# Ten unused TensorE products left out of the attention units of a hybrid decoder layer

## The chip, the cores and the metric

The kernel runs on one core of a Trainium2 chip. The metric is the device time of one execution in microseconds (us). The kernel before took 753.51 us, the median of three runs (752.41 to 755.99). The span of its profiled execution, from the first to the last instruction, is 749.3 us.

## The reference

One layer: a combined input projection feeds a state-space head group (S5) and a sparse attention head group; both are normalised, joined and projected out; a gated MLP with a short convolution follows. Cut to the part around the change:

```python
def one_block(args):                       # one block of 128 queries
    s_h = jnp.einsum('bthd,bsd->bths', qib, ki)
    s_idx = jnp.einsum('bths,bth->bts', jax.nn.relu(s_h), wib)
    _, sel = lax.top_k(s_idx, topk)        # 128 keys of up to 512
    logits = jnp.einsum('bthd,btkhd->bhtk', qb, kg) * scale
    p = jax.nn.softmax(logits, axis=-1)
    return jnp.einsum('bhtk,btkhd->bthd', p, vg)
...
y_ssm = _s5_mixer(u, ...)                  # diagonal state space, gelu, gated by a 512x512 product
y_mix = jnp.concatenate([_rmsnorm(y_ssm, ...), _rmsnorm(y_attn, ...)], axis=-1)
h = h + g1[:, None, :] * (y_mix @ w_out)
hn2 = _modulate(_rmsnorm(h, norm_ffn), sh2, sc2)
h = h + g2[:, None, :] * ((jax.nn.gelu(gate) * val) @ w_down)
```

The sequence has 512 positions, the model 1024 channels, and there are 8 heads of 64.

## The kernel before, in words

Each engine has its program written out by hand, in an order fixed in the source, and semaphores tie the engines together. The large float32 products (lines 1601 to 1603, `mm3`) are split into a high and a low part of each operand. Up to about 180 us the program makes the projections. Then come 32 attention units, number i being head i % 8 of query tile i // 8, with 128, 256, 384 or 512 keys by tile. After them come the output projection (to about 360 us) and the MLP.

A unit has these steps: TensorE forms the logits (line 1816, into bank i % 2); VectorE adds the mask and takes the maximum (line 1368); ScalarE takes the exponential (line 962); TensorE turns the probabilities (line 1606, `flip`, into bank 2 + i % 2); ScalarE copies them back (line 935); TensorE multiplies them with the values (line 1836). VectorE's program also holds, between its two mask steps of a pair of units and those of the next, the rounds of the top-k search for a later tile (lines 1309 and 1312), parts of S5, and later the sums of the modulation vectors (line 1175). The table `S5_AT` puts the S5 stages among the units: "u" (turns of 64x64), "lags" (line 1927), "states" (line 1917), "y" (lines 1946 and 1951), "g" and "glu".

TensorE's loop takes two units at a time: the logits of units i and i + 1, and then, for the units i - 2 and i - 1, the S5 stage, the turn of the probabilities, and the values of the unit before. The logits of unit i wait until VectorE has read those of unit i - 2 from the same bank (`logit_ready`). The table `KEEP_BUSY` names ten even units, 8 to 22 and 28 and 30. Ahead of the logits of such a unit TensorE makes one more product (line 1969, `keep_busy`): the identity as the one operand, 512 columns of the turned keys as the other, into the bank of the turned probabilities. It waits for no semaphore, sets none, and nobody reads what it writes before the next turn overwrites it. Two more of this sort of product in other places (`warm`, line 1642, in the first 40 us; lines 2062 and 2068 in `up_first`, behind 340 us) are not touched.

Of the kernel before, what the change touches and what calls it, by code (L numbers as in the profile page):

```python
# [96 lines left out]
    return ((t,),) * ROUNDS.get(i, 0), ((t,) if i < 24 and i % HEADS == 7 else ())  # L97


KEEP_BUSY = (*range(8, 24, 2), 28, 30)  # L100
OUT_BANK = ((4, 6, 7, 5), (0, 1, 2, 3))
LOGITS = 3
LO_DVE = U_GLU
# [2 lines left out]
def layer(nc, x, c, positions, w_ada, b_ada, norm_mix, w_in, ssm_log_dt, ssm_a_re, ssm_a_im, ssm_b_re,  # L106
# [6 lines left out]
    with ExitStack() as ctx:  # L113
        def sb(name, shape, dt=F32, stack=ctx):
            return stack.enter_context(nc.sbuf_tensor(name, shape, dt))
# [4 lines left out]
        bank = [ctx.enter_context(nc.psum_tensor(f"bank{i}", [P, 512], F32)) for i in range(8)]  # L120
# [6 lines left out]
        ident = sb("ident", [P, P])  # L127
# [23 lines left out]
        def cut(a, *shape):  # L151

            n = math.prod(shape)
            assert a + n <= ARENA
            v = arena[:, a:a + n]
            names = "abcd"[:len(shape)]
            if len(shape) == 1:
                return v
            return v.rearrange(f"p ({' '.join(names)}) -> p {' '.join(names)}",
                               **{k: s for k, s in zip(names, shape)})  # L160
# [3 lines left out]
        q_t, k_t = cut(0, 4, SEQ), cut(2048, 4, SEQ)  # L164
# [1431 lines left out]
        def _(pe):  # L1596
            T = nc.tensor
# [213 lines left out]
            def logits(i):  # L1811
                t, h = i // HEADS, i % HEADS
                hp = slice(64 * (h % 2), 64 * (h % 2) + 64)
                if i >= 2:
                    pe.wait_ge(S["logit_ready"], i - 1)
                T.matmul(bank[i % 2][:, 0:KEYS[t]], q_t[hp, h // 2, t * P:(t + 1) * P], k_t[hp, h // 2, 0:KEYS[t]],
                         start=True, stop=True).then_inc(S["logit_mm"], 1)

            def turn_probs(i):
                t = i // HEADS  # L1820
                pe.wait_ge(S["prob_ready"], i + 1)
                if i >= 2:
                    pe.wait_ge(S["prob_t_ready"], i - 1)
                for s in range(t + 1):
                    ins = flip(bank[2 + i % 2][:, s * P:(s + 1) * P], prob[:, i % 2, s * P:(s + 1) * P])
                ins.then_inc(S["prob_turned"], 1)

            def values(i):
                t, h = i // HEADS, i % HEADS
                pe.wait_ge(S["prob_t_ready"], i + 1)  # L1830
                if h == 0:
                    pe.wait_ge(S["proj_read"], 16 + t + 1)
                if h == 0 and t >= 2:
                    pe.wait_ge(S["y_attn_ready"], t - 1)
                for s in range(t + 1):
                    ins = T.matmul(bank[4 + t % 2][:, h * HD:(h + 1) * HD], prob_t[:, i % 2, s * P:(s + 1) * P],  # L1836
                                   v_tok[:, s, h * HD:(h + 1) * HD], start=(s == 0), stop=(s == t))
                ins.then_inc(S["pv_done"], 1)
# [125 lines left out]
                    ins = flip(bank[b][:, t * P:(t + 1) * P], y[:, t, (k % 4) * P:(k % 4 + 1) * P])  # L1964
                ins.then_inc(S["mix_t"], 1)

            def keep_busy(i):

                T.matmul(bank[2 + i % 2][:], ident[:], k_t[:, 0, :], start=True, stop=True)

            for i in range(0, ATT_UNITS + 4, 2):
                if i < ATT_UNITS:
                    if i in KEEP_BUSY:
                        keep_busy(i)
                    logits(i)
                    logits(i + 1)
                for j in (i - 2, i - 1):
                    if j in S5_AT:
                        s5(*S5_AT[j])
                    if 0 <= j < ATT_UNITS:  # L1980
                        turn_probs(j)
                    if 0 <= j - 1 < ATT_UNITS:
                        values(j - 1)
# [199 lines left out]
```

## Time and profile before

| | us |
|---|---|
| median of three runs | 753.51 |
| lowest and highest run | 752.41, 755.99 |
| span of the profiled execution | 749.3 |
| TensorE busy | 703.0 |
| VectorE busy | 458.9 |
| ScalarE busy | 338.4 |
| mean granted clock of TensorE | 0.983 |

The profiled execution is a single one; the span runs from its first to its last instruction, and the page gives no time of its own for what lies around it. The median is 4.2 us above the span. TensorE's time is start to modelled end of its instructions, so that a busy TensorE is not one at its peak. The granted clock is a share of 2.4 GHz: 1.00 is 2.4 GHz, 0.50 is 1.2 GHz, and a value between them is a stretch that holds some of both.

### The profile page before, as it was taken

The page shows a single profiled execution, that of the slowest core. Times are in us where ns is not written, and L with a number is a line of the kernel's source. Part 1 is how long each engine was busy: PE and PEld are TensorE (multiplying, and loading weights), DVE is VectorE, ACT ScalarE, POOL GpSimd, SP SyncE. Part 2 cuts the span into 40 slices and gives each one's busy share as a digit, 9 for nine tenths or more (in the row PEclk, how much of TensorE's full clock was granted, in tenths as well). Part 3 has the DMA queues.
Part 4 walks back from the last instruction along what each step waited for, and adds up shares of the span by engine and source line. Part 5 has one row for each costly group of instructions (what it writes and reads, how often), then busy time and mean ns, then how long its engine had stood idle before and what let it go on. Part 6 is the DMA issues. An engine that isn't in the chain of part 4 may idle for free.

```text
span 749.3 us, 9903 instructions
## 1 busy us (share of the span) xinstructions
PE 703.0 (94%) x3570; PEld 554.8 (74%) x3570; DVE 458.9 (61%) x817; ACT 338.4 (45%) x508; POOL 262.9 (35%) x212
## 2 busy tenths in 40 slices
PE   0799999999888899999899999999999999999997
PEld 0587777777575566888797888888878887888886
DVE  2868987976999899798615866654554544000005
ACT  4534456746522756423665445455545454122120
POOL 2002899329904200000023343443342443443440
PEclk9999999999879999999998999999999999999999
DMA  8952221260373738645603323313313313313302
GB/s 335 380 138 74 66 103 57 85 197 1 39 75 73 234 133 314 246 170 194 227 1 113 99 69 112 112 59 109 111 58 112 110 59 113 108 61 112 113 1 112
DMA packets 63081, 91.46 MB, mean 122 GB/s; under 512 B 12011, under 2 KB 41475, under 8 KB 62980
## 3 DMA queue, kind: packets, MB, share of 16 engines
q1 hardware_dynamic: 59520, 89.44, 37.2%
q10 hardware_dynamic: 3523, 1.54, 0.7%
q8 instruction: 22, 0.36, 0.2%
q14 instruction: 16, 0.12, 0.1%
HBM read 86.28 MB, written 4.69 MB: 121 GB/s over the span
## 4 chain that ended last, share of the span: by engine, by line
PE 68%; DVE 24%; ACT 3%; issue 3%; DMA 1%; SPq 0%; DVEq 0%; ACTq 0%
PE bank L1601 20%; PE bank L1603 20%; PE bank L1602 20%; DVE arena L1175 4%; DVE w_lo L1161 2%; PE bank L1606 2%; DVE arena L1312 2%; DVE arena L1151 2%; DVE stat L1309 2%; PE bank L1951 1%; DMA xh<-in_x 1%; PE bank L1946 1%; DVE arena L1368 1%; PE bank L1836 1%; ACT w_hi L697 1%
## 5 line engine op out<-in xcount | busy, mean ns | idle before, releaser
L502 POOL TENSOR_TENSOR w_lo<-w_raw,w_hi 128x2048 fp32r<-128x2048 f32 x33 | 152.1, 4612 | 349.5 <-ACT w_hi L1047 280.3
L1601 PE MATMUL bank<-act_hi,w_hi 128*128 128x512 f32 (+2 forms) x384 | 148.1, 386 | 2.1 <-DVE conv L1557 1.6
L1602 PE MATMUL bank<-act_lo,w_hi 128*128 128x512 f32 (+2 forms) x384 | 147.0, 383 | 0.0
L1603 PE MATMUL bank<-act_hi,w_lo 128*128 128x512 f32 (+2 forms) x384 | 146.8, 382 | 0.0
L1601 PE MATMUL bank<-w_hi,act_hi 128*128 128x512 f32 x240 | 98.5, 410 | 1.1 <-DVE act_lo L1201 1.1
L1603 PE MATMUL bank<-w_hi,act_lo 128*128 128x512 f32 x240 | 94.9, 396 | 0.0
L1602 PE MATMUL bank<-w_lo,act_hi 128*128 128x512 f32 x240 | 94.6, 394 | 0.0
L697 ACT ACTIVATE w_hi<-w_raw 128x2048 fp32r<-128x2048 f32 x26 | 49.8, 1913 | 84.8 <-PE bank L1603 82.1
L1601 PEld LDWEIGHTS bank<-act_hi,w_hi 128*128 128x128 f32 x384 | 73.1, 190 | 17.9 <-issue 2.0
L1553 DVE SCALAR_TENSOR_TENSOR conv<-bank,vec_cols,conv 128x511 f32<-128x511 f32 x44 | 33.0, 749 | 86.2 <-ACT conv L1057 85.8
L1603 PEld LDWEIGHTS bank<-act_hi,w_lo 128*128 128x128 f32 x384 | 73.1, 190 | 14.4
L1602 PEld LDWEIGHTS bank<-act_lo,w_hi 128*128 128x128 f32 x384 | 73.2, 191 | 14.3 <-issue 0.2
L1601 PE MATMUL bank<-w_hi,ff_hi 128*128 128x512 f32 x176 | 69.6, 396 | 0.0
L1603 PE MATMUL bank<-w_hi,ff_lo 128*128 128x512 f32 x176 | 69.5, 395 | 0.0
L1602 PE MATMUL bank<-w_lo,ff_hi 128*128 128x512 f32 x176 | 69.5, 395 | 0.0
L1591 DVE TENSOR_TENSOR up<-bank,arena 128x512 f32<-128x512 f32 x8 | 5.5, 692 | 103.5 <-PE bank L1603 103.5
L1057 ACT ACTIVATE conv<-bank,vec_cols 128x512 f32<-128x512 f32 x44 | 33.9, 778 | 72.9 <-PE bank L1603 72.9
L1606 PE MATMUL bank<-ident,arena 128*128 128x128 f32 (+1 forms) x252 | 39.5, 281 | 20.4 <-DVE arena L1139 11.4
L1601 PEld LDWEIGHTS bank<-w_hi,act_hi 128*128 128x128 f32 x240 | 45.2, 188 | 17.1 <-issue 7.5
L1566 DVE TENSOR_TENSOR up<-conv 128x512 f32<-128x512 f32 x22 | 42.4, 1964 | 19.8 <-ACT conv L1064 19.7
L1603 PEld LDWEIGHTS bank<-w_hi,act_lo 128*128 128x128 f32 x240 | 45.1, 188 | 10.6
L1606 PEld LDWEIGHTS bank<-ident,arena 128*128 128x128 f32 (+1 forms) x252 | 29.2, 144 | 31.9 <-issue 15.2
(318 smaller groups left out, 1176.8 us busy)
## 6 DMA issues: line engine op xcount, KB each, us to landing
w_raw<-in_w_up SPq DMA_DIRECT2D x44, 512.0 KB, 4.6
arena<-in_w_ada SPq DMA_DIRECT2D x18, 1024.0 KB, 8.2
w_raw<-in_w_down SPq DMA_DIRECT2D x22, 512.0 KB, 4.2
w_raw<-in_w_in SPq DMA_DIRECT2D x10, 1024.0 KB, 5.1
xh<-in_x SPq DMA_DIRECT2D x8, 512.0 KB, 7.4
w_raw<-in_w_out SPq DMA_DIRECT2D x4, 1024.0 KB, 10.1
arena<-in_w_ada SPq DMA_DIRECT2D x2, 2048.0 KB, 11.3
arena<-lag_dram SPq DMA_DIRECT2D x16, 128.0 KB, 5.5
```

What stands on the lines that cost most here:

```text
L502: nc.gpsimd.tensor_tensor(w_lo[:, slot, 0:width], w_raw[:, slot, 0:width], w_hi[:, slot, 0:width].bitcast(F32), ALU.subtract).then_inc(S[" ...
L697: nc.scalar.activation(w_hi[:, slot(n), 0:width], w_raw[:, slot(n), 0:width], ACT.Copy).then_inc(S["hi_ready"], 1)
L1057: nc.scalar.activation(conv[:, q, :], bank[q][:], ACT.Identity, scale=vec_cols[:, bass.ds(j * 2 + (C_W2 + f), 1)], bias=vec_cols[:, bass.d ...
L1151: ins = V.scalar_tensor_tensor(dst, src, silu_c[:, k:k + 1], dst, ALU.mult, ALU.add)
L1161: V.tensor_tensor(w_lo[:, slot(n), :], w_raw[:, slot(n), :], w_hi[:, slot(n), :].bitcast(F32), ALU.subtract).then_inc(S["lo_ready"], 1)
L1175: link(V.scalar_tensor_tensor(acc, src, s, acc, ALU.mult, ALU.add), "ada_used" if k == 3 else "dve_chain")
L1553: V.scalar_tensor_tensor(conv[:, q, 1:], bank[q][:, 0:SEQ - 1], vec_cols[:, bass.ds(j * 2 + (C_W1 + f), 1)], conv[:, q, 1:], ALU.mult, ALU ...
L1566: V.tensor_tensor(up32[:, q, :], conv[:, q, :], conv[:, 2 + q, :], ALU.mult).then_inc(S["ff32_ready"], 1)
L1601: T.matmul(dst, lhs_hi, rhs_hi, start=start, stop=False)
L1602: T.matmul(dst, lhs_hi, rhs_lo, start=False, stop=False)
L1603: return T.matmul(dst, lhs_lo, rhs_hi, start=False, stop=stop)
L1606: return T.matmul(dst, src, ident[at:at + n, at:at + n], is_transpose=True, start=True, stop=True)
```

## The change

The table `KEEP_BUSY`, the function `keep_busy` and its call are taken out. TensorE's program is otherwise the same, and so are those of the other engines; line numbers behind the table are one lower, and behind the function seven lower.

```diff
-KEEP_BUSY = (*range(8, 24, 2), 28, 30)
 OUT_BANK = ((4, 6, 7, 5), (0, 1, 2, 3))
...
-            def keep_busy(i):
-
-                T.matmul(bank[2 + i % 2][:], ident[:], k_t[:, 0, :], start=True, stop=True)
-
             for i in range(0, ATT_UNITS + 4, 2):
                 if i < ATT_UNITS:
-                    if i in KEEP_BUSY:
-                        keep_busy(i)
                     logits(i)
                     logits(i + 1)
```

TensorE's program of the kernel before around unit 16, where L1917 is the stage "states", L1816 the logits of units 16 and 17, and L1946 and L1951 the stage "y":

```order
L1917 MATMUL bank<-up,s_mem 64x64 x32
L1606 MATMUL bank<-ident,arena 128x128 x2
L1836 MATMUL bank<-arena 128x64 x2
L1969 MATMUL bank<-arena,ident 128x512
L1816 MATMUL bank<-arena 128x384 x2
L1946 MATMUL bank<-arena,s_mem 64x128 x2
```

The same place of the changed kernel, with its line numbers:

```order
L1916 MATMUL bank<-up,s_mem 64x64 x32
L1605 MATMUL bank<-ident,arena 128x128 x2
L1835 MATMUL bank<-arena 128x64 x2
L1815 MATMUL bank<-arena 128x384 x2
L1945 MATMUL bank<-arena,s_mem 64x128 x2
```

Only the row of L1969 is gone. The last two of the ten stand ahead of the logits of units 28 and 30; before:

```order
L1836 MATMUL bank<-arena 128x64 x4
L1969 MATMUL bank<-arena,ident 128x512
L1816 MATMUL bank<-arena 128x512 x2
L1606 MATMUL bank<-ident,arena 128x128 x4
L1836 MATMUL bank<-arena 128x64 x4
L1606 MATMUL bank<-ident,arena 128x128 x4
L1836 MATMUL bank<-arena 128x64 x4
L1969 MATMUL bank<-arena,ident 128x512
L1816 MATMUL bank<-arena 128x512 x2
```

And after:

```order
L1835 MATMUL bank<-arena 128x64 x4
L1815 MATMUL bank<-arena 128x512 x2
L1605 MATMUL bank<-ident,arena 128x128 x4
L1835 MATMUL bank<-arena 128x64 x4
L1605 MATMUL bank<-ident,arena 128x128 x4
L1835 MATMUL bank<-arena 128x64 x4
L1815 MATMUL bank<-arena 128x512 x2
```

Nothing between them changes its place.

## Rows read from the trace of the kernel before

**Rows 1.** The page, busy tenths in 40 slices of the span.
```profile
DVE  2868987976999899798615866654554544000005
PEclk9999999999879999999998999999999999999999
```

**Rows 2.** All records of line 1969 (two of each product): least, median, longest ns.
```profile
L1969 PE MATMUL bank<-arena,ident x20: 592/648/1167, 189.2 to 294.0; 128*128 128x512 f32 x20
```

**Rows 3.** VectorE in order of time: start, duration, what, [idle before <- releaser].
```profile
192.38 0.48 DVE L1368 CUSTOM_DVE_ANT_0 arena<-bank,arena,stat 128x256 f32<-128x256 f32 x1 [0.91 <-PE bank L1816]
...
249.79 0.62 DVE L1368 CUSTOM_DVE_ANT_0 arena<-bank,arena,stat 128x384 f32<-128x384 f32 x1 [0.87 <-DVE arena L1312]
...
263.01 1.29 DVE L1424 TENSOR_TENSOR act_lo<-bank,act_hi 128x512 fp32r<-128x512 f32 x2 [1.48 <-ACT act_hi L883]
...
296.01 0.75 DVE L1368 CUSTOM_DVE_ANT_0 arena<-bank,arena,stat 128x512 f32<-128x512 f32 x1 [0.55 <-PE bank L1816]
```

**Rows 4.** The chain that ended last, where line 1969 is in it: start, us.
```profile
189.37 1.81 PE bank L1969 x2
...
247.90 0.91 PE bank L1969 x2
```

**Rows 5.** Stretches: length, busy PE, PEld, DVE, ACT, POOL; granted clock; DMA share, GB/s.
```profile
202.00:203.00 1.00, 0.07 (x1) 0.00 (x0) 0.93 (x4) 0.00 (x0) 0.92 (x2) 1.00 0.80 173
203.00:204.00 1.00, 0.00 (x0) 0.00 (x0) 0.96 (x4) 0.00 (x0) 1.00 (x1) 1.00 1.26 154
205.00:206.00 1.00, 1.00 (x9) 0.88 (x9) 0.97 (x2) 0.00 (x0) 0.00 (x0) 0.84 1.26 119
209.00:210.00 1.00, 1.00 (x10) 1.00 (x9) 0.93 (x3) 0.00 (x0) 0.00 (x0) 0.95 1.16 114
219.00:220.00 1.00, 1.00 (x15) 1.00 (x14) 1.00 (x2) 0.42 (x1) 0.00 (x0) 0.67 0.98 208
226.00:227.00 1.00, 1.00 (x7) 0.64 (x5) 1.00 (x2) 0.00 (x0) 0.92 (x2) 0.92 1.24 110
188.00:189.00 1.00, 1.00 (x11) 1.00 (x9) 0.93 (x4) 0.80 (x4) 0.92 (x2) 0.81 0.00 0
184.00:188.00 4.00, 2.31 (x18) 1.74 (x19) 2.87 (x12) 4.00 (x10) 3.92 (x3) 1.00 0.00 0
260.00:264.00 4.00, 2.31 (x20) 2.13 (x19) 2.45 (x6) 3.24 (x6) 0.00 (x0) 1.00 1.01 378
```

**Rows 6.** TensorE in order of time, "states" at either clock, and idle ahead of "u".
```profile
211.17 2.10 PE L1917 MATMUL bank<-s_mem 128*64 128x64 f32 x64
...
218.82 1.57 PE L1606 MATMUL bank<-ident,xh 64*128 64x64 f32 x16 [1.79 <-DVE arena L1407]
...
221.69 3.74 PE L1917 MATMUL bank<-up,s_mem 128*64 128x64 f32 x64
```

**Rows 7.** TensorE in order of time, around unit 16 and the stage "y".
```profile
226.39 1.08 PE L1969 MATMUL bank<-arena,ident 128*128 128x512 f32 x2
227.47 1.31 PE L1816 MATMUL bank<-arena 64*128 64x384 f32 x4
230.36 0.44 PE L1946 MATMUL bank<-arena,s_mem 128*64 128x128 f32 x4 [1.58 <-DVE s_mem L1407]
```

**Rows 8.** TensorE in order of time, around units 22, 28 and 30.
```profile
261.61 1.42 PE L1606 MATMUL bank<-ident,arena 128*128 128x128 f32 x11 [1.53 <-ACT arena L977]
...
293.56 1.08 PE L1969 MATMUL bank<-arena,ident 128*128 128x512 f32 x2
294.85 1.79 PE L1816 MATMUL bank<-arena 64*128 64x512 f32 x4 [0.22 <-DVE stat L1368]
```

**Rows 9.** The chain of waits, first and last TensorE pieces between 294 and 306 us.
```profile
294.85 1.79 PE bank L1816 x4
...
305.47 0.45 PE bank L1606 x4
```

**Rows 10.** The chain of waits, last TensorE piece of "y".
```profile
246.56 0.58 PE bank L1951 x8
```

## The prediction

> **What bounds the kernel now.** The change touches only the attention units, from about 180 to 306 us, so I read the page's slices first. There the reader is to see VectorE at seven to nine tenths, where from 400 us on it stands at four to six, and TensorE's granted clock below nine tenths in two slices [rows 1]. VectorE is the engine that the units wait for, and TensorE has slack, so a product taken from it pays only where VectorE waits. The second view is all records of line 1969: 20 records for ten products, median 648 ns each [rows 2]. In a row one product keeps TensorE 1.08 us at full clock [rows 7, 8], and 1.81 us of the chain at half clock in the one at 189 us [rows 4]. Together that is 9 x 1.08 + 1.8 = 11.5 us of TensorE's time, which is not what the change can give. The third view is VectorE in order of time: in 120 us it waits with a gap worth naming only at 192.38 (0.91 us), 249.79 (0.87), 263.01 (1.48) and 296.01 (0.55) [rows 3]. The chain that ended last holds two of the ten products, ahead of the first two of these waits, with 1.81 and 0.91 us [rows 4]. The fourth view is the granted clock by stretch. It is at its lower level, 1.2 GHz, from 205.7 to 209.1 us (0.84 in the first slice is 0.32 us at the lower level, 0.95 in the last is 0.10 us) and from 219.3 to 226.2 (0.67 and 0.92), that is for 3.4 and 6.8 us [rows 5].
>
> **The change part by part.** It removes ten products and nothing else; it adds no wait and moves nothing.
>
> 1. *Unit 8 (189 us).* VectorE waits 0.91 us for the logits of units 8 and 9, which stand right behind a product of 1.81 us [rows 3, 4]. Without it the wait goes: -0.9. What is late next is VectorE itself, so the other 0.9 us of the product is slack. Bounds: -0.91 and 0 (if another step in front of the logits takes the place).
>
> 2. *Units 10, 12 and 14.* VectorE never waits between 192.4 and 249.8 us [rows 3], so neither the products nor a clock that falls a little earlier cost or give anything while TensorE's work is ready 2 us ahead: 0.
>
> 3. *Units 16 and 18, and the stage "y".* The logits of unit 18 stand behind 0.91 us of a product, and VectorE waits 0.87 us for them [rows 3, 4]. Taken alone that is -0.87. But between unit 16 and 18 TensorE has the stage "y", from 230.36 to 247.1 us, in one piece [rows 7, 10], and it begins when VectorE lets it, after 1.58 us of idle [rows 7]. The product of unit 16 stood ahead of logits that VectorE released only as they started, so its 1.08 us turn into idle time: of 226.4 to 230.4 us TensorE is then busy 1.31 us [rows 7]. What did it do before the clock fell elsewhere? Ahead of 205.7 it was idle for two slices but for 0.07 us; ahead of 219.3 for 1.79 us; ahead of 188.6 (0.81 in that slice) it was busy 2.31 us of 4. But 260 to 264, also 2.31 of 4, was followed by no fall [rows 5, 6]. 1.31 of 4 lies on the side of the falls, so I take it that "y" begins at 1.2 GHz. The price: "states", the same 64 instructions, takes 2.10 us at full and 3.74 us at half clock [rows 6], so a stretch of 3.4 us at half clock does 3.4 x 2.10 / 3.74 = 1.9 us of work and loses 1.5 us; one of 6.8 us loses 3.0. TensorE thus ends "y" 1.5 us later, and gains 1.0 by the product of unit 18: +0.5. Bounds: -0.87 (no fall) and +2.0 (the long stretch).
>
> 4. *Units 20 and 22.* Their products are followed by 1.53 us of idle at 261.61, where TensorE waits for the gelu on ScalarE [rows 8]. The logits of unit 22 wait for VectorE less than 1.08 us, so nearly the whole product of unit 22 becomes idle time, some 2.5 us in all. If the clock falls there, the first turns for "g" are late by half a microsecond and VectorE's wait of 1.48 us at 263.01 [rows 3] grows by it; the gate products behind are needed by VectorE only some us later. I take +0.5; bounds 0 and +1.5.
>
> 5. *Units 28 and 30, the end of the units.* The product at 293.56 ends just before the logits of unit 30 may start, at 294.85, after 0.22 us of waiting for VectorE [rows 8]. Its removal gives nothing, and that of unit 28 only lets TensorE arrive 1.08 us earlier. The idle time ahead of 294.85 becomes 0.22 + 1.08 + 1.08 = 2.4 us, longer than that ahead of the falls at 205.7 and 219.3. From 294.85 to 305.92 the chain is on TensorE throughout [rows 9]. I take one stretch of 3.4 us at half clock, priced as above: +1.5. Bounds: 0 and, with all 11.1 us at half clock and the ratio of "states", 11.1 x (3.74 / 2.10 - 1) = +8.7; nearest the rows is 1.5, since of the two falls of rows 5 one lasted 3.4 us and ended in dense work, as would this one with its 512-column logits.
>
> The Trainium skill says that transposes are not counted as TensorE activity the way matmuls are ("TensorE: Matmul & The Clock Gate", Part 4: PE-mode transpose). No row settles it: in 260 to 264 us, where the turns of line 1606 take 1.42 us [rows 5, 8], the clock did not fall, which speaks against it. By the rule alone the end of the units, nearly half of it turns, would stay at the lower clock, which is the second rival below.
>
> The sum: -0.9 + 0 + 0.5 + 0.5 + 1.5 = +1.6 us. The profiled span goes from 749.3 to 750.9, and with the 4.2 us by which the median stands above the span the time is 755.1 us.
>
> **The rivals.**
>
> *The clock stays up everywhere.* Then only steps 1 and 3 act, -0.91 and -0.87: 753.5 - 1.8 = 751.7 us. For it speaks that 1.53 and 1.58 us of idle were survived, and that earlier products pull the work behind them forward and may split the idle time. Against it, the idle of 2.4 us ahead of unit 30 is longer than any that was survived.
>
> *The lower clock stays through "y" or through the end of the units.* This is the one on the slower side: with fewer dense products in it a stretch at 1.2 GHz is not ended, as 219.3 to 226.2 was not for 6.8 us, in small products and 64x64 turns [rows 5, 6]. Place: "y" and 294.85 to 305.92, where TensorE is the chain. Price: "y" +2.0 instead of +0.5, the end +3.0 to +6 instead of +1.5, with the other terms the same: -0.9 + 2.0 + 0.5 + 3.0 = +4.6, up to +7.6, so 758 to 761 us; I put it at 759. It decides once the end holds more than two such stretches, or both places one long one each. For it: turns and 64-column products fill these 11 us. Against: the logits of unit 30, 1.79 us of 512 columns [rows 8].
>
> *The products are hidden anyway.* Neither the products nor the clock matter: the waits of 0.9 us are taken up by something else and no fall is added: 753.5 us. That the chain runs over two of the products speaks against it.
>
> **How the numbers follow.** Forecast (one short fall in each place) 0.46, the clock stays up 0.18, products hidden 0.09, the lower clock stays 0.27. The predicted time is the forecast's, 755.1 us. The range leaves out the far ends of both sides: 751.5 to 759.5 us; the forecast's own is 753 to 757.5. 0.5% is 3.8 us, which is about what a measurement of this kernel can tell from no change: 749.7 and 757.3 are the limits. Slower by more than that is the last rival and the upper end of the forecast: 0.30. Faster is only a part of the first rival in which the phases fall well: 0.05. The rest, 0.65, is within 0.5%.
>
> **What the profile after would show.** Step 1: VectorE's wait at 192 us gone. Step 2: none between there and "y". Step 3: granted clock 0.5 in the slices from about 229 us, the first groups of "y" at about twice their time, and the wait ahead of unit 18's mask between 0.9 and 2 us. Step 4: a low clock at about 261 us. Step 5: idle of over 2 us ahead of unit 30's logits and a clock of 0.5 right behind. The forecast is wrong if the clock is 1.00 in 229 to 233 and 293 to 298 us, if a stretch at 0.5 there lasts beyond 4 us, or if anything outside 180 to 320 us differs by more than a microsecond.

## The result and the profile after

The changed kernel takes 760.27 us (median of 4 runs, 759.21 to 768.88) against 754.75 us (median of 4) of the kernel before: ratio 1.010, 95% interval 1.0056 to 1.0144, so 0.6 to 1.4% slower. Ten further runs gave 761.11 against 754.12, ratio 1.0069 (1.0037 to 1.0101). Here and below medians are over all runs of a kernel, while ratios leave out those over 1.5% above its fastest (three of ten in the kernel without unit 28's product, at most two in any other set), so the two can differ a little. The forecast was 755.1 us, with 759.5 as the upper end. The time lies within the second rival's 758 to 761.

The profiled execution of the changed kernel spans 757.2 us and took 759.21 us; 2.0 us lie around the span. The same 2.0 us hold for every run, so the profiled execution of before, with its span of 749.3 us, was itself 2.2 us faster than the median of 753.51.

The page, busy tenths in 40 slices, answers to [rows 1]:

```profile
DVE  2869987976999898488735757655545555000005
PEclk9999999999688998699999999999999999999999
```

VectorE's line has a slice of four tenths from 303 to 322 us, where before the slice from 300 to 318 had seven, and TensorE's clock has two low places: one from 189 to 246 us, deeper than before, and one from 284 to 322 us that before has not.

VectorE in order of time, with its waits, answers to [rows 3]:

```profile
252.22 0.62 DVE L1367 CUSTOM_DVE_ANT_0 arena<-bank,arena,stat 128x384 f32<-128x384 f32 x1 [1.65 <-issue]
...
265.84 1.29 DVE L1423 TENSOR_TENSOR act_lo<-bank,act_hi 128x512 fp32r<-128x512 f32 x2 [1.49 <-ACT act_hi L882]
...
299.81 0.75 DVE L1367 CUSTOM_DVE_ANT_0 arena<-bank,arena,stat 128x512 f32<-128x512 f32 x1 [1.50 <-PE bank L1815]
...
312.19 0.20 DVE L1375 RECIPROCAL stat<-stat 128x8 f32<-128x8 f32 x1 [6.77 <-PE bank L1835]
```

The wait for unit 8's logits is gone, that for unit 18's has grown from 0.87 to 1.65 us, and the one for the last values, line 1375, stands at 6.77 us. Before, the same step waited 1.29:

```profile
302.91 0.20 DVE L1376 RECIPROCAL stat<-stat 128x8 f32<-128x8 f32 x1 [1.29 <-PE bank L1836]
```

TensorE in order of time at that place, first the last work of unit 27 and then all of the end, answers to [rows 8]:

```profile
294.64 1.00 PE L1835 MATMUL bank<-arena 128*128 128x64 f32 x8
297.70 2.74 PE L1815 MATMUL bank<-arena 64*128 64x512 f32 x4 [2.05 <-DVE stat L1367]
300.37 1.11 PE L1605 MATMUL bank<-ident,arena 128*128 128x128 f32 x4
301.28 1.80 PE L1835 MATMUL bank<-arena 128*128 128x64 f32 x8
...
308.63 3.52 PE L1835 MATMUL bank<-arena 128*128 128x64 f32 x16
311.94 1.91 PE L1605 MATMUL bank<-ident,arena 128*128 128x128 f32 x8
```

And the granted clock (third column from the end) in stretches of 1 us, answering to [rows 5]:

```profile
296.00:297.00 1.00, 0.00 (x0) 0.00 (x0) 0.96 (x2) 0.00 (x0) 0.00 (x0) 1.00 0.04 16
297.00:298.00 1.00, 0.30 (x1) 0.31 (x2) 1.00 (x3) 0.32 (x1) 0.00 (x0) 0.68 0.27 29
298.00:299.00 1.00, 1.00 (x3) 0.69 (x3) 0.31 (x2) 1.00 (x4) 0.00 (x0) 0.50 0.70 131
...
313.00:314.00 1.00, 1.00 (x6) 0.98 (x5) 0.35 (x2) 0.80 (x2) 0.00 (x0) 0.50 0.03 8
314.00:315.00 1.00, 1.00 (x3) 0.29 (x2) 0.90 (x2) 1.00 (x3) 0.00 (x0) 0.79 0.78 111
```

TensorE idles 2.05 us, falls to 1.2 GHz at 297.4 us and stays there until 314.4, for 17 us. From 297.70 on it is busy without a gap, first with the 512-column logits of units 30 and 31 (2.74 us), then with turns and 64-column products at nearly twice their time (eight records of line 1835: 1.80 us against 1.00 ahead of the fall).

Where the time went, by the starts of VectorE's mask step of each unit in the two profiles: 0.3 us less up to unit 6, 1.17 less at unit 8, 1.65 more at unit 10, unchanged to unit 16, 2.43 more at unit 18, 2.83 more from unit 20 to 28, 3.80 more at unit 30, and 10.45 more just behind the units (the second group of line 1433, at 317.12 against 306.67). At 393 us the execution of before fell to 1.2 GHz and that of the changed kernel didn't, which gave back 2.7 us. So of a difference of 7.9 us in the spans, 7.6 came at the end of the units, 2.8 between units 8 and 10, and 1.2 at "y" and the pair of units behind it; 0.9 was won at unit 8, 2.7 at 393 us, and 0.3 ahead of the units; the 0.2 us that are left lie elsewhere.

### The profile page after: what moved, and what is told of

The parts are those of the page before. It is cut to its first block, busy times and chain, and to the rows that moved or that the text cites. A ratio compares the mean times of both kernels' runs of the same rounds, so it can differ in the third digit from the quotient of the medians.

```text
span 757.2 us, 9863 instructions
## 1 busy us (share of the span) xinstructions
PE 703.3 (93%) x3550; PEld 560.5 (74%) x3550; DVE 461.8 (61%) x817; ACT 338.3 (45%) x508; POOL 262.9 (35%) x212
## 4 chain that ended last, share of the span: by engine, by line
PE 68%; DVE 22%; ACT 4%; issue 3%; DMA 1%; SPq 0%; ACTq 0%; DVEq 0%
PE bank L1600 20%; PE bank L1602 20%; PE bank L1601 20%; DVE arena L1174 4%; PE bank L1605 3%; DVE w_lo L1160 2%; DVE arena L1150 2%; DVE arena L1311 1%; PE bank L1950 1%; DVE stat L1308 1%; PE bank L1835 1%; PE bank L1945 1%; DMA xh<-in_x 1%; PE bank L1815 1%; ACT w_hi L696 1%
## 5 line engine op out<-in xcount | busy, mean ns | idle before, releaser
L1605 PE MATMUL bank<-ident,arena 128*128 128x128 f32 (+1 forms) x252 | 42.1, 295 | 21.9 <-DVE arena L1138 11.4
L1605 PEld LDWEIGHTS bank<-ident,arena 128*128 128x128 f32 (+1 forms) x252 | 31.4, 152 | 34.4 <-issue 14.7
```

Of the source, the lines that this page charges most:

```text
L1605: return T.matmul(dst, src, ident[at:at + n, at:at + n], is_transpose=True, start=True, stop=True)
```

## The experiments

All are compared with runs of the kernel before on the same chip. Single runs of one kernel lie several us apart (before: 748.5 to 760.6 us in one set of 31 runs, 748.8 to 765.8 in another), so that a difference under 0.4% isn't told from none. The time at 1.2 GHz that is given over all runs is worked out from each run's mean granted clock and span. In each, A is the theory that the loss sits at the end of the units, by the low clock.

**Two products alone, and eight alone.** With `KEEP_BUSY = (28, 30)`:

```diff
-KEEP_BUSY = (*range(8, 24, 2), 28, 30)
+KEEP_BUSY = (28, 30)
```

> Only the last two of the ten products are kept. Theory A (the loss sits at the end of the units: TensorE idles 2 us ahead of unit 30's logits, falls to 1.2 GHz and finds no way back through the turns and 64-column products): the stretch at 1.2 GHz from 297 to 314 us is gone, VectorE's wait for the last values (6.8 us) shrinks to about 1.3, and the kernel takes 1 to 3 us more than before (what units 8 and 16 add stays). Theory B (each product is worth about the same, whatever its place): 8 of 10 are out, so 5 to 6 us more than before. Theory C (nothing but the late steps of VectorE at 197 us matters): 2 to 3 us more than before and the low clock at the end as in the changed kernel.

Measured: 757.58 us, ratio 1.005 (1.002 to 1.008), 3.2 us more than before. The stretch at the end is gone, which speaks against C, and the wait for the last values is 1.29 us. This is just above A's 1 to 3 us; B had said 5 to 6.

With the last two left out and the other eight kept:

```diff
+KEEP_BUSY = (*range(8, 24, 2),)
```

> Only the last two of the ten products are left out. Theory A: 5 to 8 us more than before, with 1.2 GHz from about 294 us for over 10 us, and everything up to 290 us as before. Theory B: 1 to 2 us more than before. Theory C: no difference within 1 us.

Measured: 763.02 us (4 runs), ratio 1.0124 (1.008 to 1.0169), 8.6 us more. Its profiled execution was its fastest run. There too TensorE idled, for 2.08 us, and fell, but the stretch lasted only 6.8 us, from 298.9 to 305.7, and ended among turns and 64-column products, with no 512-column work since the logits at 299.43 to 302.2. The clock where it fell and where it came back:

```profile
298.00:299.00 1.00, 0.00 (x0) 0.00 (x0) 0.96 (x2) 0.00 (x0) 0.00 (x0) 0.95 0.00 0
305.00:306.00 1.00, 1.00 (x9) 1.00 (x7) 0.90 (x5) 0.30 (x1) 0.00 (x0) 0.64 1.03 387
```

The same kernel was run again:

> The kernel without the last two products once more, as its first comparison had four runs alone. Theory A: 5 to 8 us more than before, VectorE's wait for the last values 3 us (6.8 us at the lower clock) or 6.8 us (17 us). If the first result (8.6 us) was a chance of four runs: under 3 us.

Measured: 760.18 us (6 runs), ratio 1.0091 (1.0054 to 1.0127), 6.8 us more, and in the profile 17 us at 1.2 GHz and a wait of 6.78 us for the last values. Leaving out two of the ten products costs as much as leaving out all ten (5.5 and 7.0 us). B, which had 1 to 2 us here, is out. That everything up to 290 us would be as before did not hold: the logits of unit 30 start at 299.43 and 298.10 us against 294.85, though the program is the same up to there, so a single pair of profiles differs by 3 to 5 us on its own. VectorE at that place, without the last two products, second profile:

```profile
312.59 0.20 DVE L1376 RECIPROCAL stat<-stat 128x8 f32<-128x8 f32 x1 [6.78 <-PE bank L1836]
```

**The changed kernel again.**

> The changed kernel once more, for the spread of its runs and a second profile. Theory A (the end of the units makes the loss): 6 to 9 us more than before, and again a stretch at 1.2 GHz that begins within 1 us of unit 30's logits. Theory A says nothing of its length, which was 17 us in the first profile and 6.8 us in the one profile without the last two products: more than 6 us here. The rival that the first profile was a chance: a median within 3 us of before.

Measured: 761.11 us, 7.0 us more. The profiled execution, 766.74 us, again has 17 us at 1.2 GHz, from 305.0 to 322.1 us, after 1.88 us of idle, and again a wait of 6.77 us. The first profile was no chance.

**Which of the two.** First without the product of unit 28, then without that of unit 30.

```diff
+KEEP_BUSY = (*range(8, 24, 2), 30)
```

> Only the product of unit 28 is left out; that of unit 30 stays and covers 1.1 us of the idle time right ahead of unit 30's logits. If the length of the gap ahead of 294.8 us decides (2.4 us without both, 1.3 with one), the clock stays up and the kernel is within 1.5 us of before. If both products are needed as work, it falls as without both: 5 us or more.

```diff
+KEEP_BUSY = (*range(8, 24, 2), 28)
```

> Only the product of unit 30 is left out; TensorE comes as late as before to the end of unit 27's values, and idles 1.3 us ahead of unit 30's logits. By the length of the gap alone: as the kernel without the product of unit 28, within 1.5 us of before. If what counts is a filler directly in front of the logits, this one falls and that one doesn't: 4 to 8 us more here.

Measured: 755.02 us, ratio 0.9979 (0.9937 to 1.0021), and 753.19 us, ratio 0.9990 (0.9948 to 1.0033). Either one is enough; which doesn't matter. The profiled execution of the kernel without unit 28's product took 761.03 us, but not by a low clock at this place. The logits of unit 30 without unit 30's product, and at the same place of the kernel without unit 28's:

```profile
294.18 1.79 PE L1816 MATMUL bank<-arena 64*128 64x512 f32 x4 [1.15 <-DVE stat L1368]
```

```profile
302.85 1.08 PE L1969 MATMUL bank<-arena,ident 128*128 128x512 f32 x2
305.09 1.79 PE L1816 MATMUL bank<-arena 64*128 64x512 f32 x4 [1.16 <-DVE stat L1368]
```

1.15 and 1.16 us of idle, and 1.79 us for the logits, the time at full clock. In the eight profiles with both products and the three with one, the clock holds through the end of the units; in the six with neither TensorE idles 1.85 to 2.09 us there, and the clock fell in five of them (the sixth is the next experiment's).

Over all runs of a kernel the median time at 1.2 GHz is 27 us before, 28 and 27 without one of the last two products, 43 and 40 without both (the other eight kept), and 55 in the changed kernel. The kernel that keeps only the last two has 43 us as well, yet is 3.2 us slower than before and not 7 to 9: what a stretch costs depends on where it lies.

**Is it the thin work that keeps the clock down?** The last two are left out and one product is put behind the logits of unit 30, into the stretch.

```diff
+KEEP_BUSY = (*range(8, 24, 2), 32)
...
             for i in range(0, ATT_UNITS + 4, 2):
+                if i in KEEP_BUSY:
+                    keep_busy(i)
                 if i < ATT_UNITS:
-                    if i in KEEP_BUSY:
-                        keep_busy(i)
                     logits(i)
```

> The products of units 28 and 30 are left out, and one is put after them, where the loop would form the logits of a unit 32, in the middle of the stretch at 1.2 GHz. If the stretch lasts because nothing dense is in it, this product (about 2 us at half clock) ends it early: the low clock lasts 3 to 7 us and the kernel takes 3 to 6 us more than before, less than without it (8.6). If the work in it doesn't matter, it only adds 1 to 2 us: 9 to 11 us more than before.

Measured: 757.64 us, ratio 1.0049 (1.0011 to 1.0087), 3.5 us more than before and 3 to 5 less than without the product. The profile doesn't show why: after 1.88 us of idle the clock didn't fall in this execution. Over the ten runs the median time at 1.2 GHz is 34 us, against 43 and 40 without the product. The same product was then put into the changed kernel, alone:

```diff
+KEEP_BUSY = (32,)
```

> The changed kernel with one product alone, put behind the logits of unit 30 into the stretch at 1.2 GHz. If the stretch lasts because nothing dense is in it, the clock falls as in the changed kernel (idle of 1.9 to 2.1 us ahead of unit 30's logits) and is back after 3.4 to 7 us; VectorE's wait for the last values is 3 to 5 us, and the kernel takes 2 to 4 us less than the changed one. If the kind of work doesn't matter, 17 us at the lower clock again and 1 to 2 us more than the changed one.

Measured: 760.86 us (4 runs), ratio 1.0102 (1.0042 to 1.0163), no less than the changed kernel. Here the clock fell, and the profile shows what the product does. TensorE in order of time, then the clock:

```profile
307.03 2.02 PE L1969 MATMUL bank<-arena,ident 128*128 128x512 f32 x2
308.84 1.05 PE L1606 MATMUL bank<-ident,arena 128*128 128x128 f32 x4
309.70 1.03 PE L1836 MATMUL bank<-arena 128*128 128x64 f32 x8
```

```profile
306.00:307.00 1.00, 1.00 (x6) 1.00 (x6) 1.00 (x3) 0.97 (x3) 0.00 (x0) 0.50 1.06 408
309.00:310.00 1.00, 1.00 (x8) 1.00 (x7) 0.00 (x0) 0.07 (x1) 0.00 (x0) 0.63 0.00 0
310.00:311.00 1.00, 1.00 (x11) 1.00 (x11) 0.00 (x0) 0.53 (x1) 0.00 (x0) 1.00 0.00 0
```

The clock is back at 309.7 us, 0.7 us behind the product's end, after 10.2 us instead of 17, and the next products with the values and the turns behind them run at full clock (line 1836: 1.03 us). But the product itself takes 2.0 us of the chain and the wait for the last values is still 5.89 us: 0.9 us won, less than was expected and not to be seen in the time. That the product ended the stretch is likely but not shown: one profile has 10.2 us against three of 17, and the median time at 1.2 GHz is 50 us against 55, but without the last two products a stretch also ended after 6.8 us with no such product in it. As a remedy it is worth little here.

**One product in place of ten.**

```diff
+KEEP_BUSY = (30,)
```

> The changed kernel with the product of unit 30 alone. By the length of the gap (1.2 us instead of 2) the clock doesn't fall at the end: VectorE's wait for the last values 1.3 us, and the kernel 2 to 4 us above before, as with the last two products alone (3.3). If more than this product was needed, 6 us or more above before.

Measured: 758.55 us (7 runs), ratio 1.0056 (1.0022 to 1.0090), 5.2 us more. The clock holds at the end (wait 1.30 us), as A has it, but 5.2 is between its range and the rival's. With the 3.2 us of the kernel that keeps both of the last, it shows that the eight earlier products are worth something too, some 3 to 5 us together. That and the 7 to 9 us of the last two don't add up to the 5.5 to 7 us of the whole change; the intervals are wide enough to cover that gap, and whether the parts add up is open.

**Unit 8, and units 16 and 18.**

```diff
+KEEP_BUSY = (*range(10, 24, 2), 28, 30)
```

> Only the product of unit 8 is left out. Theory C (taking away VectorE's wait of 0.9 us at 192 us shifts its small additions of line 1387 from the gap between two GpSimd instructions into one of 2 us, and they are held until it ends): logits of unit 8 0.9 us earlier, those of unit 10 about 1.7 to 2 us later than before, the two records of line 1387 at 1.0 and 2.0 us instead of 0.2 each, in all 1.5 to 2 us more than before. Theory D (the shift was a matter of the clock): the records of line 1387 stay at 0.2 us and the kernel is within 1 us of before.

Measured: 756.18 us, 1.8 us more, ratio 1.0020 (0.9986 to 1.0053): the size that C had, but the interval holds no change. In the profile the records of line 1387 are long, as C said. They are long in all six profiles without unit 8's product and in five of the nine that keep it, so a share of the product in it is neither shown nor excluded.

```diff
+KEEP_BUSY = (8, 10, 12, 14, 20, 22, 28, 30)
```

> Only the products of units 16 and 18 are left out. Theory A2 (the stage y then begins at 1.2 GHz): granted clock 0.5 from about 229 us, VectorE's wait for unit 18's logits grows from 0.87 us to 1.5 to 3 us, 0.5 to 2 us more than before. Rival (the clock holds, since in the changed kernel it had been low for long before): clock 1.00 through y, the wait gone, 0.9 us less than before.

Measured: 754.50 us, ratio 1.0004 (0.9972 to 1.0035). The profile has 1.2 GHz from 230.5 to 237.3 us, and 2.19 us of wait for unit 18's logits, as A2 said. But of the eleven profiles of kernels that keep both products eight have a stretch at 1.2 GHz in "y" too (without unit 28's product 237.2 to 244.0, wait 3.63 us). In those eight unit 18's mask step comes 12.0 to 13.9 us behind unit 16's, in the three others 11.0, and in the six profiles without the two products 11.8 to 12.7: the price is paid with and without them.

**More products, and the small additions.** The next two keep all ten and put three more where TensorE idles ahead of an S5 stage, the second also five short ones ahead of the second MLP group.

```diff
                 for j in (i - 2, i - 1):
+                    if j in (12, 14, 20):
+                        keep_busy(j)
                     if j in S5_AT:
```

> All ten products stay, and three more stand ahead of the S5 stages of units 12, 14 and 20, where TensorE idles 1.8, 1.6 and 1.5 us before it. Theory A (a product is worth what it keeps the clock up for, and costs nothing in idle time): fewer stretches at 1.2 GHz between 216 and 270 us, VectorE's waits at 250 and 263 us stay below 1 and 1.5 us, 0.5 to 2 us less than before. Rival (before has the clock where it matters, and the product only stands in front of the stage): 0 to 1.5 us more.

```diff
             up_first()
+            for _ in range(5):
+                T.matmul(bank[7][:], act_hi[:, 0, 0:P], act_hi[:, 0, :], start=True, stop=True)
```

> As the kernel with three more products, and five products of 0.22 us in the 1.6 us of idle time at the start of the second MLP group (392.3 to 394.2 us), where the clock fell in two of the first profiles and made the group 2.7 us longer. Theory A: the fall at 393 us doesn't come, 0.5 to 1.5 us less than the kernel with three more alone, on the mean of runs. Rival: no difference, since the fall there comes in some executions alone or not through this gap.

Measured: 756.60 us, ratio 1.0026 (0.9992 to 1.0059), and 753.29 us, ratio 0.9983 (0.9944 to 1.0022). Three more alone win nothing (if anything they cost, as the rival has it). The second differs from it by 3.3 us in the medians, near the limit of what these runs can tell, and no fall stands in its profile after 275 us. But six of the fifteen profiles of kernels without the five short products have no fall there (393 to 405 us) either, so that these keep the clock up is not shown.

> The kernel before, with the two small additions of line 1387 for the first half moved from VectorE to GpSimd, behind its 2-us instructions. Theory C (they are held on VectorE until a GpSimd instruction that reads SBUF ends, 2.3 to 2.8 us in seven of ten profiles): VectorE's time between the logits of units 8 and 10 is never over 11 us, the median 1 to 2.3 us below before. Rival: the late additions were in cover, the median the same within 0.7 us.

```diff
-                sp.wait_ge(S["lag_d_added"], 2 * half + 2)
+                sp.wait_ge(S["lag_d_added" if half else "lag_d_pool"], 2)
...
             weigh_lags(1)
+            for i in range(2):
+                pool.wait_ge(S["lags_ready"], i + 1)
+                g = 4 * i
+                G.tensor_tensor(lags[0][:, g:g + 4, 0, :], lags[0][:, g:g + 4, 0, :], d_eye[:, g:g + 4, :],
+                                ALU.add).then_inc(S["lag_d_pool"], 1)
...
-                        if stage == "lags" and back == 1:
+                        if stage == "lags" and back == 1 and half == 1:
```

Measured: 752.39 us, ratio 0.9985 (0.9944 to 1.0025): the median is 1.9 us lower, the interval holds no change; inconclusive in time. In the profile unit 10's mask step comes 0.3 us nearer to unit 8's than before.

> The additions on GpSimd, the three more products and the five ahead of the second MLP group together. If all three mechanisms are as told, 2 to 5 us less than before and the narrowest spread of runs. If they only trade with one another, within 1 us of before.

Measured: 751.31 us (11 runs), ratio 0.9936 (0.9902 to 0.9970). With the additions on GpSimd, the three more products and the five ahead of the MLP group, this is the one version faster than both kernels, by 0.3 to 1.0%; nine of its eleven runs lie within 749.4 to 751.6 us. Over its runs the median time at 1.2 GHz is 16 us, against 27 before. How much each of the three parts gives was not told apart.

## Why the prediction was wrong

At the end of the units the mechanism was the predicted one; the size of that term was wrong, and with it the choice among the rivals. Of the smaller terms step 1 was right, step 3 had the right place and too small a size, and steps 2 and 4 were wrong.

*Step 5 failed.* It forecast idle of 2.4 us ahead of unit 30 (measured 2.05 and 1.88), the lower clock from there on (it fell at 297.4 us, the logits start at 297.70) and then "one stretch of 3.4 us at half clock", at +1.5. Measured is a stretch of 17 us and +7.6 us in the profiles, +6.8 and +8.6 us in the two sets of runs without the last two products alone. Its own upper bound was +8.7. The reason given for the small value was that the stretch would end in dense work "with its 512-column logits". These logits stood at the head of the stretch, took 2.74 us instead of 1.79, and did not end it: it lasted 14 us more. The rows shown had both cases, a fall that ended after 3.4 us in the 128-column products of line 1927 and one that lasted 6.8 us through turns and 64-column products; the end of the units, after the logits, is all of the second kind. The rows did not bound the stretch at 3.4 us, and with TensorE the chain throughout each further one cost its full price. Why it lasts 17 us in three profiles and 6.8 in a fourth is open.

The reading of VectorE's waits also left out the one of 1.29 us at 302.91, which is the one that grew to 6.77. The sum did not use it, since step 5 took the chain there from TensorE's side.

*The rival was the outcome.* It had a chance of 0.27 and 759 us. Its condition, a lower clock through 294.85 to 305.92, came in full length in three of the four profiles with neither of the last two products and nothing in their place. At "y", its other place, the stretch lasted 6.8 us.

*Step 1* was right as a mechanism: unit 8's logits came 0.87 us earlier, against -0.91 forecast. In time, leaving out this product alone wins nothing: 1.8 us more, with an interval that holds no change.

*Step 2* was wrong in the profile, by 2.8 us between units 8 and 10, though "VectorE never waits" was true: two additions of 32x64 took 3.15 us instead of 0.37, which is counted as busy and not as a wait. It is no effect of the change alone, since it stands in five of the nine profiles of kernels that keep unit 8's product; in the six without it, it always does.

*Step 3*: the clock fell at 229.1 us, as forecast, and stayed low to 235.9, for 6.8 us instead of 3.4; unit 18's mask step came 0.78 us later and unit 20's another 0.40, so +1.2 against +0.5, within the bounds. But leaving out just these two products cost nothing (ratio 1.0004), since kernels that keep them fall there too (eight profiles of eleven). The single profile of before, with no fall there, was taken as the rule.

The changed kernel in stretches of 1 us, where the fall and the return stand:

```profile
229.00:230.00 1.00, 0.88 (x3) 0.88 (x4) 1.00 (x6) 0.87 (x3) 0.77 (x1) 0.55 0.27 25
235.00:236.00 1.00, 1.00 (x10) 0.34 (x8) 1.00 (x2) 0.00 (x0) 0.00 (x0) 0.54 0.00 0
```

*Step 4* did not come: no fall at 261 us in this execution, a wait of 1.49 us at the gelu against 1.48 before, and the same distance of 2.8 us from unit 20 to unit 28, so 0 against +0.5. The second profile has a fall at 267.5 us. The 0.40 us at unit 20 lie ahead of this place; in all six profiles without the products of units 16 and 18, one of which keeps that of unit 20, unit 20's mask step comes 8.1 us behind unit 18's, and 7.7 in all others.

*The base.* The profile of before was a lucky execution, 2.2 us faster than the median; the forecast added its sum to the median, so this did not move it. Terms that this execution has escaped, the fall at "y" and the long additions, look like the change's effect in a comparison of two profiles.

## What to carry to other kernels

A product that nobody reads can be worth more than its time: ask what TensorE does in the microsecond ahead of the next piece of chain and, above all, what it does behind it. Ahead of a run of turns and narrow products that the next stage waits for, a fall lasted 17 us in three profiles, until 512-column products came, and 6.8 us in one; so price it up to that whole run, and not with the shortest stretch at hand. And where single executions differ by more than the effect, the landmarks of one pair of profiles show where time can go, and only left-out-alone kernels with many runs show where it went.

## What the runs showed of the hardware

The two small VectorE additions of line 1387, each of two SBUF operands, wait inside their own duration for GpSimd. Before, they came just where one GpSimd instruction ends and the next starts. VectorE, then GpSimd, of the kernel before:

```profile
198.19 0.37 DVE L1387 TENSOR_TENSOR arena<-arena 32x64 f32<-32x64 f32 x2
```

```profile
195.98 2.37 POOL L537 TENSOR_TENSOR arena<-arena,up 128x1024 f32<-128x1024 f32 x1
198.43 2.03 POOL L538 TENSOR_TENSOR arena<-arena 128x1024 f32<-128x1024 f32 x1
```

And of the changed kernel:

```profile
197.06 3.15 DVE L1386 TENSOR_TENSOR arena<-arena 32x64 f32<-32x64 f32 x2
```

```profile
195.66 2.36 POOL L536 TENSOR_TENSOR arena<-arena,up 128x1024 f32<-128x1024 f32 x1
198.10 2.03 POOL L537 TENSOR_TENSOR arena<-arena 128x1024 f32<-128x1024 f32 x1
```

The first (1.04 us) ends as GpSimd's first instruction does, the second (2.02 us) as its second. Of the fifteen profiles in which VectorE makes these additions, they are long (1.2 to 3.2 us together) in eleven and short (0.36 to 0.46) in four, before among them. Each held one ends within 0.1 us of the end of a GpSimd instruction, and the four short pairs all begin less than 0.3 us ahead of such an end. The Trainium skill says that VectorE and GpSimd share a pair of SBUF ports as an exclusive lock, taken also by a VectorE operation with two SBUF inputs against a GpSimd operation that reads SBUF, and that the loser is blocked for the whole instruction ("SBUF — State Buffer", SBUF: two separate sides). The rows agree: 0.2 us of work ends with the 2-us instruction beside it.

The clock did not fall by the idle time alone. After 1.88 us it fell in one execution and held in another, of a kernel that differs behind this place only in one product. After 0.86 to 1.16 us at this place it held (three profiles). And in the kernels compared here the stretches at 1.2 GHz lasted 3.4, 6.8, 10.2 or 17 us, the longest through the logits, turns and narrow products without a gap in TensorE's work. The Trainium skill's statement that transposes do not count as TensorE activity the way matmuls do ("TensorE: Matmul & The Clock Gate", Part 4: PE-mode transpose) fits the 17 us, in which turns and 64-column products alternate, but does not by itself account for the profile in which the clock came back after 6.8 us in the same work; no run here separates the turns from the narrow products.
